# Taking the last 16 tokens out of the expert down products and computing their dots from gathered rows

## The chip, the cores and the metric

The kernel runs on one core of one Trainium2 chip. The metric is the device time of one execution in microseconds (us); the figure shown for a kernel is the median of several runs. A difference of about 0.3% (5.2 us) is what a measurement of this kernel can tell from none.

## The reference

The program is two transformer blocks over 256 tokens of width 1024 (S = 256, D = 1024). All that the change touches lies in the last part, a layer of product-key experts:

```python
def _peer(h, w_q, subkeys, w_down, w_up):
    ...
        v, i = lax.top_k(s, PEER_TOPK)
        cand = (v[..., 0, :, None] + v[..., 1, None, :]).reshape(B, TB, PEER_HEADS, PEER_TOPK * PEER_TOPK)
        ...
        tv, tj = lax.top_k(cand, PEER_TOPK)
        eidx = jnp.take_along_axis(cidx, tj, axis=-1)
        w = jax.nn.softmax(tv, axis=-1)
        u = w_down[eidx]
        a = jax.nn.gelu(jnp.einsum('btd,btpkd->btpk', hblk, u).astype(jnp.float32))
        vv = w_up[eidx]
        return jnp.einsum('btpk,btpkd->btd', (w * a).astype(hblk.dtype), vv)
```

Each token picks 16 of 16,384 experts in each of 8 heads. Of every picked expert its down row (1024 values) is multiplied with the token, the result goes through gelu, is weighted, and scales the expert's up row.

## The kernel before

**Dense products instead of gathers.** The 16,384 experts are 128 tiles of 128 experts. For every tile the kernel computes the down products of all 256 tokens (experts on the partitions, tokens on the columns), so the array `WA` (128 x 128 tiles x 256 tokens) comes to hold gelu(down product) times routing weight, zero where a token did not pick the expert. Then the up products of all 128 tiles are summed in PSUM.

**Weights as pieces.** Down and up rows arrive as a stream of 529 pieces of 128 x 1024 float32 (512 KB), loaded by SyncE into a ring of three buffers (`load_piece`, L178). Each piece is split in two reduced-precision float32 parts: ScalarE copies the high half (`split_high`, L192), and another engine subtracts it from the piece for the low half (`split_low`, L199): GpSimd in the lead described below, VectorE elsewhere. Three pairs of split buffers (AHEAD = 3) stand between these engines and TensorE, and the split of piece q + 3 waits until TensorE has used piece q. A product of two split operands is three matmuls: high x high, high x low, low x high.

**The stages of the expert layer**, in order of time:

1. Key scores. TensorE computes queries and scores, VectorE takes the top 16 of each half.
2. The lead: tiles 0 to FIRST - 1 (FIRST = 36), `lead_tile` (L2359). Per tile `down` (L2312) issues 8 x 3 matmuls of 256 columns (the lines L273, L274 and L277 of `mm3`), ScalarE splits the high half of the tile three ahead and applies gelu into `WA`, and GpSimd makes the low half. The tiles 6 to 29 are in a loop that VectorE takes no part in. VectorE meanwhile finds each token's 16 best pairs and their expert numbers (L2460 to L2516), then waits for ScalarE's exponential (L2518), whose place in ScalarE's own order is behind the loop. Three tiles before the end TensorE turns expert numbers and weights by token (`turn_route`, L2528).
3. The routing steps: 64 steps of 4 tokens (ROUTES = 64). Per step VectorE makes two one-hot arrays (`onehots`, L2557 and L2558), ScalarE weights one (`weights_in`, L2566), TensorE multiplies them (`route_product`, L2575), and ScalarE and VectorE write the resulting weights into `WA` for those 4 tokens. Beside it each step does the down products of one more tile in a wider form, `down_wide` (L2327): per k one matmul of 512 columns (the high half against both parts of the tokens, L2337) and one of 256 (L2341); `whole_tile` (L2352) adds the two halves.
4. The pairs: 28 tiles (100 to 127), each with `down_wide`, gelu and weighing, followed by the up product of another tile (12 matmuls of 512 columns).
5. The up products of the last 100 tiles, then the final norm.

The order on each engine is as written in the program; every engine works its own list in order and waits on semaphores. Before the routing steps the lists read:

```python
    for u in range(FIRST - BODY, FIRST):
        ...
        lead_tile(u, None)
    onehots(1)
    V.wait_ge(s_low, q1 + AHEAD)
```

Of the kernel before, what the change touches and what calls it, by code (L numbers as in the profile page):

```python
# [28 lines left out]
U32 = mybir.dt.uint32  # L29
ALU = mybir.AluOpType  # L30
# [25 lines left out]
FIRST = 36  # L56
TB = 4
ROUTES = S // TB
# [59 lines left out]
def build(nc, a, out):  # L118
# [2189 lines left out]
    I16f = carve(NT, 2 * PH, TOPK)  # L2308
    s_gelu = nc.alloc_semaphore("gelu_done")
    q0 = pos["q"] + 2 * PH  # L2310

    def down(q, s, u, n, first=False):  # L2312

        if not first:
            T.wait_ge(s_gelu, n + (u - 2))

        def products(h, l):
            for k in range(KD):
                last = mm3(bank[4 + u % 3][:, 0:S], (h[:, k * P:(k + 1) * P], l[:, k * P:(k + 1) * P]),
                           (xh[:, k, :], xl[:, k, :]), k == 0, k == KD - 1)  # L2320
            return last
        piece_ops(q, s, products)
# [4 lines left out]
    def down_wide(q, s, v, n):  # L2327

        T.wait_ge(s_gelu, n + (v - 2))
        b = bank[4 + v % 3]  # L2330

        def products(h, l):
            for k in range(KD):
                ks = slice(k * P, (k + 1) * P)

                def both_parts(stop):
                    return T.matmul(b[:, :], h[:, ks], xs[:, k, :, :].rearrange("p a t -> p (a t)"), start=k == 0, stop=stop,  # L2337
                                    skip_group_check=True)

                def high_part(stop):  # L2340
                    return T.matmul(b[:, 0:S], l[:, ks], xh[:, k, :], start=False, stop=stop, skip_group_check=True)  # L2341
# [10 lines left out]
    def whole_tile(g, v, n):  # L2352

        b = bank[4 + v % 3]
        C.activation(g[:, :], b[:, S:2 * S], ACT.Copy).then_inc(s_right, 1)
        V.wait_ge(s_right, n + (v - FIRST + 1))
        V.tensor_tensor(g[:, :], b[:, 0:S], g[:, :], ALU.add).then_inc(s_whole, 1)

    def lead_tile(u, i):  # L2359
        n = 0 if i is None else i * BODY  # L2360
        down(q0 + u, n, u, n, first=i is None and u < 3)
        split(q0 + u + AHEAD, i, low=G)
        C.wait_ge(s_used, n + (q0 + u + 1))
        row = WA[:, u, :] if i is None else WA[:, bass.ds(n + u, 1), :].rearrange("p a t -> p (a t)")
        C.activation(row, bank[4 + u % 3][:, 0:S], ACT.Gelu_apprx_tanh).then_inc(s_gelu, 1)
# [29 lines left out]

    for st in range(2 * PH + 3):
# [46 lines left out]
    with nc.Fori(1, FIRST // BODY - 1, engines=(ENG.PE, ENG.Activation, ENG.Pool)) as i:  # L2443
# [55 lines left out]
    places = (order, place)  # L2499
    dve.wait(ci)  # L2500
# [3 lines left out]
    for w in range(2):  # L2504
        for t in range(NT):
# [9 lines left out]
    W3 = Wt.rearrange("p t h k -> p (t h) k")  # L2515
    s1 = dve.did(V.tensor_tensor(W3, TV, TV[:, :, 0:1].broadcast_to([P, NT * PH, TOPK]), ALU.subtract))  # L2516
    act.wait(s1)
    e_ = act.did(C.activation(Wt, Wt, ACT.Exp))  # L2518
    dve.wait(e_)
    m = dve.did(V.tensor_reduce(wsum, Wt, AX.X, ALU.add))  # L2520
    dve.wait(m)
    m = dve.did(V.reciprocal(wsum, wsum))
    dve.wait(m)
    for t in range(NT):
        wd = dve.did(V.tensor_tensor(Wt[:, t, :, :], Wt[:, t, :, :], wsum[:, t, :].unsqueeze(2).broadcast_to([P, PH, TOPK]),
                                     ALU.mult))

    def turn_route(n_, src, ready, dst):  # L2528

        pe.wait(ready)  # L2530
        for t in range(NT):
            last = T.transpose(bank[1 + n_][:, t * P:(t + 1) * P], src[:, t, :, :].rearrange("p h k -> p (h k)"), ident)
        r_ = pe.did(last)
        act.wait(r_)
        return act.did(C.activation(dst[:, :], bank[1 + n_][:, 0:S], ACT.Copy))
# [46 lines left out]
    def route_copy(g):  # L2582

        lo = FIRST + min(g + 1, ROUTES - 1)
        C.wait_ge(s_wp, g + 1)
        C.activation(WA[:, lo:NE, TB * g:TB * g + TB], by_tile(g)[:, lo:NE, :], ACT.Copy).then_inc(s_wc, 1)

    def route_multiply(g):
# [3 lines left out]
        V.wait_ge(s_wc, g + 1)  # L2592
        V.wait_ge(s_gelu, hi)
# [9 lines left out]
    def late_gelu(g):  # L2603
# [456 lines left out]
```

## Time and profile before

| what | us |
| --- | --- |
| median of 3 runs | 1719.74 |
| lowest and highest run | 1718.23, 1723.38 |
| span of the profiled execution (first to last instruction) | 1718.3 |
| TensorE busy in it | 1692.9 |
| VectorE, ScalarE, GpSimd busy in it | 1283.4, 970.7, 234.7 |

The profile gives the span as the profiled execution's own time and nothing beyond it. The median of the runs is 1.4 us above that span; this is taken for what lies around the span. In the profile PE is TensorE's matmuls, PEld its weight loads, DVE VectorE, ACT ScalarE, POOL GpSimd, SP SyncE; SPq and ACTq are the parts of SyncE and ScalarE that issue DMAs. A group of rows names line, engine, operation, what is written and read with its shape, and for waits the releaser behind an arrow. A matmul's duration overlaps the next one's, so the pace of TensorE is read from starts, not from durations.

### The profile page before, as it was taken

The page shows a single profiled execution, that of the slowest core. Times are in us where ns is not written, and L with a number is a line of the kernel's source. Part 1 is how long each engine was busy: PE and PEld are TensorE (multiplying, and loading weights), DVE is VectorE, ACT ScalarE, POOL GpSimd, SP SyncE. Part 2 cuts the span into 40 slices and gives each one's busy share as a digit, 9 for nine tenths or more (in the row PEclk, how much of TensorE's full clock was granted, in tenths as well). Part 3 has the DMA queues.
Part 4 walks back from the last instruction along what each step waited for, and adds up shares of the span by engine and source line. Part 5 has one row for each costly group of instructions (what it writes and reads, how often), then busy time and mean ns, then how long its engine had stood idle before and what let it go on. Part 6 is the DMA issues. An engine that isn't in the chain of part 4 may idle for free.

```text
span 1718.3 us, 30152 instructions
## 1 busy us (share of the span) xinstructions
PE 1692.9 (99%) x10170; PEld 1497.8 (87%) x10170; DVE 1283.4 (75%) x2549; ACT 970.7 (56%) x1798; POOL 234.7 (14%) x172
## 2 busy tenths in 40 slices
PE   9999999999999999999899999999999999999998
PEld 8888888799888887889899999999988888888886
DVE  5468877867788788867658766889987666666667
ACT  5746554566555544557455548988874544333333
POOL 2120000011100000321117883000000000000000
PEclk9999999999999999999999999999999999999999
DMA  7535767655547686444245555444446555555554
GB/s 243 189 127 156 267 206 281 212 176 202 207 146 268 217 284 243 165 160 140 82 138 170 178 180 169 140 143 148 140 143 193 187 194 185 194 195 193 190 192 146
DMA packets 86579, 317.50 MB, mean 185 GB/s; under 512 B 9664, under 2 KB 9936, under 8 KB 85968
## 3 DMA queue, kind: packets, MB, share of 16 engines
q1 hardware_dynamic: 77328, 279.48, 49.2%
q10 hardware_dynamic: 7200, 25.45, 4.0%
q0 software_dynamic: 1952, 11.25, 1.9%
q8 instruction: 61, 1.00, 0.2%
q14 instruction: 38, 0.31, 0.1%
HBM read 315.08 MB, written 1.05 MB: 184 GB/s over the span
## 4 chain that ended last, share of the span: by engine, by line
PE 69%; DVE 4%; ACT 2%; DMA 2%; issue 1%; POOL 0%; DVEq 0%; SPq 0%; ACTq 0%
PE bank L273 13%; PE bank L277 13%; PE bank L274 13%; PE bank L2337 10%; PE bank L2341 5%; PE bank L1250 4%; PE bank L2575 3%; PE bank L1254 2%; DVE wl L199 1%; DMA ada<-in_w_ada 1%; ACT wh L192 1%; PE bank L622 1%; DMA ring<-in_stream 1%; PE bank L676 1%; PE bank L699 1%
## 5 line engine op out<-in xcount | busy, mean ns | idle before, releaser
L192 ACT ACTIVATE wh<-ring 128x1024 fp32r<-128x1024 f32 x526 | 555.6, 1058 | 537.6 <-PE bank L277 356.1
L199 DVE TENSOR_TENSOR wl<-ring,wh 128x1024 fp32r<-128x1024 f32 x468 | 572.8, 1226 | 279.2 <-ACT wh L192 277.8
L273 PE MATMUL bank<-wh,xs 128*128 128x512 f32 (+1 forms) x780 | 279.5, 358 | 2.0 <-DVE wl L199 0.8
L277 PE MATMUL bank<-wh,xs 128*128 128x512 f32 (+1 forms) x780 | 275.7, 353 | 0.0
L274 PE MATMUL bank<-wl,xs 128*128 128x512 f32 (+1 forms) x780 | 275.4, 353 | 0.0
L2337 PE MATMUL bank<-xs,wh 128*128 128x512 f32 x736 | 250.8, 402 | 0.0
L1250 PE MATMUL bank<-xs,wh 128*128 128x512 f32 x672 | 212.4, 396 | 1.9 <-DVE wl L199 1.9
L273 PE MATMUL bank<-xs,wh 128*128 128x256 f32 x616 | 177.4, 288 | 0.3 <-ACT fox_v L1127 0.2
L277 PE MATMUL bank<-xs,wl 128*128 128x256 f32 x616 | 174.3, 283 | 0.0
L274 PE MATMUL bank<-xs,wh 128*128 128x256 f32 x616 | 174.2, 283 | 0.0
L199 POOL TENSOR_TENSOR wl<-ring,wh 128x1024 fp32r<-128x1024 f32 x57 | 138.4, 2430 | 262.0 <-ACT wh L192 168.4
L273 PEld LDWEIGHTS bank<-wh,xs 128*128 128x128 f32 x780 | 147.4, 189 | 25.5 <-DVE wl L199 2.9
L277 PEld LDWEIGHTS bank<-wh,xs 128*128 128x128 f32 x780 | 147.3, 189 | 20.7
L274 PEld LDWEIGHTS bank<-wl,xs 128*128 128x128 f32 x780 | 147.5, 189 | 20.3 <-issue 0.5
L2341 PEld LDWEIGHTS bank<-xs,wl 128*128 128x128 f32 x736 | 138.5, 188 | 29.3
L1254 PEld LDWEIGHTS bank<-xs,wl 128*128 128x128 f32 x672 | 126.2, 188 | 29.5
L2341 PE MATMUL bank<-xs,wl 128*128 128x256 f32 x736 | 145.1, 279 | 0.0
L1254 PE MATMUL bank<-xs,wl 128*128 128x256 f32 x672 | 132.1, 278 | 0.0
L2337 PEld LDWEIGHTS bank<-xs,wh 128*128 128x128 f32 x736 | 119.1, 189 | 1.1
L273 PEld LDWEIGHTS bank<-xs,wh 128*128 128x128 f32 x616 | 118.1, 192 | 0.8 <-ACT fox_v L1127 0.4
L274 PEld LDWEIGHTS bank<-xs,wh 128*128 128x128 f32 x616 | 118.1, 192 | 0.1
L277 PEld LDWEIGHTS bank<-xs,wl 128*128 128x128 f32 x616 | 117.9, 191 | 0.0
(505 smaller groups left out, 2849.6 us busy)
## 6 DMA issues: line engine op xcount, KB each, us to landing
ring<-in_stream SPq DMA_DIRECT2D x529, 512.0 KB, 3.4
ada<-in_w_ada ACTq DMA_DIRECT2D x48, 512.0 KB, 4.7
rows<-in_rows POOLq DMA_DIRECT2D x1, 2560.0 KB, 11.3
rows<-in_rows POOLq DMA_DIRECT2D x3, 512.0 KB, 5.2
con<-in_early POOLq DMA_DIRECT2D x1, 1374.0 KB, 14.4
x_feature_major<-in_x_fm SPq DMA_DIRECT2D x4, 256.0 KB, 5.9
x<-in_x_tm POOLq DMA_DIRECT2D x1, 1024.0 KB, 5.5
rows<-in_rows POOLq DMA_DIRECT2D x1, 1024.0 KB, 7.5
```

What stands on the lines that cost most here:

```text
L192: C.activation(wh[q % AHEAD][:, :], ring[slot][:, :], ACT.Copy).then_inc(s_high, 1)
L199: low.tensor_tensor(wl[q % AHEAD][:, :], ring[slot][:, :], wh[q % AHEAD][:, :], ALU.subtract).then_inc(s_low, 1)
L273: T.matmul(o, left[0], right[0], start=start, stop=False, skip_group_check=True)
L274: T.matmul(o, left[0], right[1], start=False, stop=False, skip_group_check=True)
L277: return T.matmul(o, left[1], right[0], start=False, stop=stop, skip_group_check=True)
L622: T.matmul(o, v[0], w[:, 0:S], start=first, stop=False, skip_group_check=True)
L676: scored = pe.did(T.matmul(b[:, P:3 * P], q[:, P:2 * P], k, start=True, stop=True, skip_group_check=True))
L1250: return T.matmul(g[:, :], h[:, ks], xs[:, k, :, :].rearrange("p a t -> p (a t)"), start=k == 0, stop=stop, skip_group_check=True)
L1254: return T.matmul(g[:, 0:S], l[:, ks], xh[:, k, :], start=False, stop=stop, skip_group_check=True)
L2337: return T.matmul(b[:, :], h[:, ks], xs[:, k, :, :].rearrange("p a t -> p (a t)"), start=k == 0, stop=stop, skip_group_check=True)
L2341: return T.matmul(b[:, 0:S], l[:, ks], xh[:, k, :], start=False, stop=stop, skip_group_check=True)
L2575: last = T.matmul(bank[g % 4][:, k * P:(k + 1) * P], oh_i[g % 2][:, k, :], oh_j[g % 2][:, k, :], start=True, stop=True, skip_group_check=True)
```

## The change

- `LIVE = 240`: every down product takes 240 columns instead of 256, the wide form 2 x 240 instead of 512. The gelus, copies and weighings of these tiles shrink alike.
- The dots of the 16 tokens left out are made another way. VectorE computes their expert numbers first (the loop over `t` runs 1, 0), ScalarE issues 8 small DMAs (`choose`) that lay out 16 tokens x 8 heads on the 128 partitions, and GpSimd issues 16 indirect DMAs (`gather`), one behind each of 16 lead tiles; each fetches 128 down rows of 4 KB from the new input `down_rows`. VectorE multiplies each gathered 128 x 1024 array with the tokens' own rows and sums along it (`chosen_dot`); TensorE has put those rows into PSUM with 8 matmuls (`own_rows`). In the routing steps 2 to 10 the 128 x 16 dots are turned by 8 DMAs of ScalarE (`dots_by_token`), go through gelu, are turned on TensorE and are multiplied into the routing weights of the 16 tokens; for these tokens the routing steps then write weight times gelu directly.
- FIRST goes from 36 to 45: nine tiles move from the pairs to the lead (19 pairs remain). The loop now covers tiles 6 to 23, tiles 24 to 44 are written out. GpSimd keeps the low halves of the whole lead.
- `onehots(1)` moves behind VectorE's wait for GpSimd's last low half.

```diff
-FIRST = 36
+FIRST = 45
+TAKEN = 16
+LIVE = S - TAKEN
+BY_POOL = 28
...
-                last = mm3(bank[4 + u % 3][:, 0:S], (h[:, k * P:(k + 1) * P], l[:, k * P:(k + 1) * P]),
-                           (xh[:, k, :], xl[:, k, :]), k == 0, k == KD - 1)
+                last = mm3(bank[4 + u % 3][:, 0:LIVE], (h[:, k * P:(k + 1) * P], l[:, k * P:(k + 1) * P]),
+                           (xh[:, k, 0:LIVE], xl[:, k, 0:LIVE]), k == 0, k == KD - 1)
...
-                    return T.matmul(b[:, :], h[:, ks], xs[:, k, :, :].rearrange("p a t -> p (a t)"), start=k == 0, stop=stop,
-                                    skip_group_check=True)
+                    return T.matmul(sides, h[:, ks], xs[:, k, :, 0:LIVE], start=k == 0, stop=stop, skip_group_check=True)
...
+    def own_rows(ready, free):
+
+        pe.wait(ready, free)
+        for k in range(KD):
+            last = T.matmul(own_ps[:, k * P:(k + 1) * P], own[:, k * P:(k + 1) * P], ident, start=True, stop=True,
+                            skip_group_check=True)
+        return pe.did(last)
...
+    def choose():
+
+        act.wait(numbered)
+        for h in range(PH):
+            C.dma_start(chosen[h * TAKEN:(h + 1) * TAKEN, :],
+                        picks_of[P - TAKEN:P, h * TOPK:(h + 1) * TOPK]).then_inc(s_chosen, 16)
+
+    def gather(r):
+
+        if r == 0:
+            G.wait_ge(s_chosen, 16 * PH)
+        if r >= len(rows_of):
+            G.wait_ge(s_dot, r - len(rows_of) + 1)
+        G.indirect_dma_start(rows_of[r % 10], None, a["down_rows"],
+                             bass.IndirectOffsetOnAxis(ap=chosen[:, r:r + 1], axis=0)).then_inc(s_row[r % 10], 16)
+
+    def chosen_dot(r):
+
+        row = rows_of[r % 10]
+        dve.wait(own_done)
+        V.wait_ge(s_row[r % 10], 16 * (r // 10 + 1))
+        V.tensor_tensor_reduce(out=row, in0=row, in1=own_ps, scale=1.0, scalar=0.0, op0=ALU.mult, op1=ALU.add,
+                               accum_out=dots[:, r:r + 1]).then_inc(s_dot, 1)
...
+    choose()
+    for u in range(LOOPED, FIRST):
...
         lead_tile(u, None)
+        if u - LOOPED < TOPK:
+            gather(u - LOOPED)
+        if u == BY_POOL + 1:
+            own_done = own_rows(own_ready, picked)
+            wd = route_weights()
+        if u >= FIRST - TOPK:
+            chosen_dot(u - (FIRST - TOPK))
+    V.wait_ge(s_low, q1 + AHEAD)
     onehots(1)
-    V.wait_ge(s_low, q1 + AHEAD)
...
+        if g == 2:
+            dots_by_token()
+        if g == 5:
+            chosen_ready = chosen_gelu()
+        if g == 8:
+            chosen_turned = chosen_turn(chosen_ready)
+        if g == 10:
+            weighed_in = chosen_weights(chosen_turned, w_in)
```

Three places in the order of the engines' lists. First GpSimd, from the end of the lead's loop (`wl` the low halves, `ring` the pieces; the line numbers of the changed kernel are up to 34 higher here). Before:

```order
L2443 COMPARE_AND_BRANCH
L199 TENSOR_TENSOR wl0<-ring0,wh0 128x1024
L199 TENSOR_TENSOR wl1<-ring1,wh1 128x1024
L199 TENSOR_TENSOR wl2<-ring2,wh2 128x1024
L199 TENSOR_TENSOR wl0<-ring0,wh0 128x1024
```

With the change:

```order
L2477 COMPARE_AND_BRANCH
L203 TENSOR_TENSOR wl0<-ring0,wh0 128x1024
L2569 DMA weighted<-in_down_rows,chosen_rows 128x1024
L203 TENSOR_TENSOR wl1<-ring1,wh1 128x1024
L2569 DMA weighted<-in_down_rows,chosen_rows 128x1024
L203 TENSOR_TENSOR wl2<-ring2,wh2 128x1024
```

The pattern goes on: 16 indirect DMAs alternate with the low halves of tiles 27 to 42, and five low halves follow without one.

Second ScalarE at the same place, before:

```order
L2443 COMPARE_AND_BRANCH
L2518 ACT_TABLE_LOAD
L2518 ACTIVATE weighted<-weighted 128x256
L192 ACTIVATE wh0<-ring0 128x1024
L2365 ACT_TABLE_LOAD
```

With the change:

```order
L2477 COMPARE_AND_BRANCH
L2602 ACT_TABLE_LOAD
L2602 ACTIVATE weighted<-weighted 128x256
L2560 DMA chosen_rows<-weighted 16x16 x8
L196 ACTIVATE wh0<-ring0 128x1024
L2379 ACT_TABLE_LOAD
```

The 8 small DMAs stand between the exponential and the high half of tile 27, and the exponential now comes after tile 23 instead of tile 29.

Third VectorE at the start of the routing steps, before:

```order
L2557 TENSOR_TENSOR onehot_i0<-keep,route_i 128x512 [waits act_done]
L2558 TENSOR_TENSOR onehot_j0<-keep,route_j 128x512
L2557 TENSOR_TENSOR onehot_i1<-keep,route_i 128x512
L2558 TENSOR_TENSOR onehot_j1<-keep,route_j 128x512
L2557 TENSOR_TENSOR onehot_i0<-keep,route_i 128x512 [waits route_product,piece_low]
```

With the change:

```order
L2646 TENSOR_TENSOR onehot_i0<-keep,route_i 128x512
L2647 TENSOR_TENSOR onehot_j0<-keep,route_j 128x512
L2577 ISA weighted,chosen_dots<-weighted,bank 128x1024 [waits gathered5]
L2577 ISA chosen_dots 128x1
L2646 TENSOR_TENSOR onehot_i1<-keep,route_i 128x512 [waits piece_low]
L2647 TENSOR_TENSOR onehot_j1<-keep,route_j 128x512
```

The one-hot arrays of step 1 now wait for GpSimd's last low half (`piece_low`); before, those of step 2 did.

## Rows read from the trace of the kernel before

**Rows 1.** The page: span, TensorE's busy time, the chain that ended last.
```profile
span 1718.3 us, 30152 instructions
PE 1692.9 (99%) x10170; PEld 1497.8 (87%) x10170; DVE 1283.4 (75%) x2549; ACT 970.7 (56%) x1798; POOL 234.7 (14%) x172
PE 69%; DVE 4%; ACT 2%; DMA 2%; issue 1%; POOL 0%; DVEq 0%; SPq 0%; ACTq 0%
```

**Rows 2.** Busy by stretch: PE, PEld, DVE, ACT, POOL; last clock, DMA share, GB/s.
```profile
961.00:1046.00 85.00, 85.00 (x712) 85.00 (x710) 61.33 (x168) 44.25 (x70) 71.12 (x30) 1.00 0.56 180
1047.00:1281.00 234.00, 234.00 (x1527) 211.85 (x1527) 205.43 (x372) 205.80 (x566) 2.85 (x2) 1.00 0.44 145
```

**Rows 3.** Timeline of GpSimd, lead: start, duration, work, count, idle before.
```profile
904.25 7.13 POOL L199 TENSOR_TENSOR wl<-ring,wh 128x1024 fp32r<-128x1024 f32 x3 [0.69 <-ACT wh L192]
...
1000.73 2.40 POOL L199 TENSOR_TENSOR wl<-ring,wh 128x1024 fp32r<-128x1024 f32 x1 [0.48 <-ACT wh L192]
1003.61 2.40 POOL L199 TENSOR_TENSOR wl<-ring,wh 128x1024 fp32r<-128x1024 f32 x1 [0.48 <-ACT wh L192]
...
1038.23 2.41 POOL L199 TENSOR_TENSOR wl<-ring,wh 128x1024 fp32r<-128x1024 f32 x1 [0.48 <-ACT wh L192]
1041.77 8.13 POOL L199 TENSOR_TENSOR wl<-ring,wh 128x1024 fp32r<-128x1024 f32 x3 [1.14 <-ACT wh L192]
```

**Rows 4.** Timeline of TensorE, among the up products and the key scores.
```profile
1285.15 0.39 PE L273 MATMUL bank<-wh,wa_high 128*128 128x512 f32 x1
...
1286.51 0.39 PE L273 MATMUL bank<-wh,wa_high 128*128 128x512 f32 x1
...
801.59 1.87 PE L1965 MATMUL bank<-kc_pair,nqT 128*128 128x30 f32 x16
```

**Rows 5.** The instructions on the tile gelu: duration min/median/max, first and last start.
```profile
L2694 ACT ACTIVATE gelu<-gelu x28: 417/418/418, 1289.4 to 1436.8; 128x256 f32<-128x256 f32 x28
```

**Rows 6.** Timeline of ScalarE at the end of the lead's loop.
```profile
1011.11 1.06 ACT L192 ACTIVATE wh<-ring 128x1024 fp32r<-128x1024 f32 x1 [1.55 <-PE bank L277]
1012.08 0.37 ACT L2365 ACTIVATE weighted<-bank 128x256 f32 x1
...
1029.35 0.37 ACT L2365 ACTIVATE weighted<-bank 128x256 f32 x1
1029.74 1.28 ACT L2518 ACT_TABLE_LOAD   x1
```

**Rows 7.** Groups by line on GpSimd: busy, mean ns, idle before.
```profile
L143 POOL DMA_DIRECT2D weighted<-in_subkeys x2 | 1.2, 579 | 0.9 <-DVE xs L429 0.9
...
L509 POOL TENSOR_TENSOR ln_rstd<-ln_var,nhalf 128x1 f32<-128x1 f32 x8 | 4.5, 558 | 3.9 <-DVE ln_var L507 3.7
...
L2066 POOL TENSOR_TENSOR ret_rstd<-ret_var,nh 128x8 f32<-128x8 f32 x1 | 1.7, 1676 | 3.6 <-DVE ret_var L2062 3.6
```

**Rows 8.** DMA issues from ScalarE: two in a row early on.
```profile
11.04 0.39 ACTq L143 DMA_DIRECT2D keep<-in_keep  x1
11.47 0.45 ACTq L143 DMA_DIRECT2D vec<-in_vec  x1
```

**Rows 9.** The instructions on the tile ada: DMA issues, and a multiply-and-sum over 1024.
```profile
L379 ACTq DMA_DIRECT2D ada<-in_w_ada x48: 334/334/339, 170.5 to 661.6; - x48
L384 DVE CUSTOM_DVE_ANT_0 ada<-ada,silu_c x48: 1215/1218/1226, 177.8 to 668.6; 128x1024 f32<-128x1024 f32 x48
```

**Rows 10.** Timeline of VectorE, choosing the experts, and the first one-hot arrays.
```profile
1014.95 2.29 DVE L2514 TENSOR_REDUCE weighted<-bank 128x128 f32<-128x2048 f32 x1
...
1049.93 0.69 DVE L2557 TENSOR_TENSOR onehot_i<-keep,route_i 128x512 f32<-128x512 f32 x1 [4.73 <-POOL wl L199]
```

**Rows 11.** Routing steps: weighting on ScalarE.
```profile
1054.99 1.27 ACT L2566 ACTIVATE onehot_j<-onehot_j,route_w 128x128 f32<-128x128 f32 x4
```

**Rows 12.** Routing steps: two consecutive routing products on TensorE.
```profile
1057.18 1.05 PE L2575 MATMUL bank<-onehot_j,onehot_i 128*128 128x128 f32 x8
1060.86 1.05 PE L2575 MATMUL bank<-onehot_j,onehot_i 128*128 128x128 f32 x8
```

More of the change, by code:

```diff
@@ L2308, in build @@
     I16f = carve(NT, 2 * PH, TOPK)
+    rows_of = [carve(D) for i in range(10)]
+    own = carve(D)
+    picks_of = carve(PH * TOPK, dt=I32)
+    chosen = sb(peer, "chosen_rows", [P, TOPK], I32)
+    dots = sb(peer, "chosen_dots", [P, TOPK])
+    dots_t = sb(peer, "chosen_dots_by_token", [TAKEN, PH * TOPK])
+    s_chosen = nc.alloc_semaphore("chosen_rows_landed")
+    s_row = [nc.alloc_semaphore(f"gathered{i}") for i in range(10)]
+    s_dot = nc.alloc_semaphore("chosen_dot_made")
+    s_dots_t = nc.alloc_semaphore("chosen_dots_turned")
     s_gelu = nc.alloc_semaphore("gelu_done")
@@ L2394, in feature_pair, with own_copies @@
         return (s_used, q + 2)
+    own_f = own.rearrange("p (k h t) -> p k h t", k=KD, h=PH)
+    def own_copies():
+        parts_of = [part[:, :, LIVE:S].unsqueeze(2).broadcast_to([P, KD, PH, TAKEN]) for part in (xh, xl)]
+        return dve.did(V.tensor_tensor(own_f, parts_of[0], parts_of[1], ALU.add))
+    own_ps = banks[:, 2 * HALF:4 * HALF]
+    def own_rows(ready, free):
[4 more added lines that the diff above has]
+        return pe.did(last)
+    dve.wait(operand["high"][KD - 1], operand["low"][KD - 1])
+    own_ready = own_copies()
     for st in range(2 * PH + 3):
@@ L2517, in build, with chosen_gelu, chosen_turn, chosen_weights @@
+    def chosen_gelu():
+        C.wait_ge(s_dots_t, 16 * PH)
+        return act.did(C.activation(dots_t[:, :], dots_t[:, :], ACT.Gelu_apprx_tanh))
+    def chosen_turn(made):
+        pe.wait(made)
+        return pe.did(T.transpose(bank[7][:, 0:TAKEN], dots_t[:, :], ident[0:TAKEN, 0:TAKEN]))
+    def chosen_weights(turned, ready):
+        dve.wait(turned, ready)
+        return dve.did(V.tensor_tensor(wT[:, LIVE:S], wT[:, LIVE:S], bank[7][:, 0:TAKEN], ALU.mult))
     act.wait(s1)
     e_ = act.did(C.activation(Wt, Wt, ACT.Exp))
-    dve.wait(e_)
@@ L2520, in build, with route_weights @@
[L2520 to L2526, printed above, removed]
+    def route_weights():
+        dve.wait(e_)
+        m = dve.did(V.tensor_reduce(wsum, Wt, AX.X, ALU.add))
+        dve.wait(m)
+        m = dve.did(V.reciprocal(wsum, wsum))
+        dve.wait(m)
+        for t in range(NT):
+            wd = dve.did(V.tensor_tensor(Wt[:, t, :, :], Wt[:, t, :, :],
+                                         wsum[:, t, :].unsqueeze(2).broadcast_to([P, PH, TOPK]), ALU.mult))
+        return wd
@@ L2641, in build @@
         if g + 1 < ROUTES:
+            if TB * (g + 1) == LIVE:
+                act.wait(weighed_in)
             weights_in(g + 1)
```

66 lines of the change are left out of this document (43 added, 23 removed).

## The prediction

> **What bounds the kernel now.** I read the page first: TensorE is busy for 1692.9 of the 1718.3 us span and holds 69% of the chain that ended last [rows 1]. So I ask of each stage whether TensorE still sets its pace, and what comes next behind it. [...] The timelines give the reserves. In the lead a low half of GpSimd starts every 2.88 us, takes 2.40, and waits 0.48 for ScalarE; run without waits, three took 7.13, so 2.38 each [rows 3]. ScalarE in turn waits 1.55 us per tile for TensorE [rows 6]. GpSimd is thus next in line in the lead, with 0.5 us to spare per tile. In the routing steps, 3.68 us apart, the weighting ends at 1056.26 and TensorE needs it at 1057.18: 0.9 us to spare [rows 11, 12].
>
> The sum is made against the span of 1718.3 us; 1.4 us are added to come to the median of 1719.74.
>
> **Columns taken away.** Six matmuls of 512 columns start within 1.36 us, 0.227 each [rows 4]; a lead tile's 24 of 256 columns fill 2.88 us, 0.120 each [rows 3]. The difference is 0.416 ns per column, over a fixed 13 ns. A tile loses 8 x 48 = 384 columns in either form, so 0.160 us, and 128 tiles lose **20.5 us**. This counts in full where TensorE sets the pace, at 2.72 us per lead tile and 3.52 per routing step.
>
> **Nine tiles moved to the lead.** A pair lasts (1436.8 - 1289.4) / 27 = 5.46 us [rows 5], of which 12 x 0.227 = 2.72 are the up product; so the wide form costs 2.74 where the lead form costs 2.88. Nine tiles add **1.3 us**.
>
> **GpSimd's 16 indirect DMAs.** The trace of before has no indirect DMA. Call g the time that one holds GpSimd. From below the nearest row is its issue of a plain DMA with 128 partitions, 0.58 us; from above its longest small operation, 8 values per partition, 1.68 us; nothing lets it come out below a plain issue, since it also has to read 128 numbers [rows 7]. I take **g = 1.0**, near the plain issue, plus most of an operation on one value per partition (0.56) for reading them [rows 7]. Even at 0.58 a tile then costs GpSimd 2.96 us against TensorE's 2.72, so GpSimd sets the pace from tile 27 on, once the stock of ready pieces is gone. When:
>
> - Tile 29's gelu runs at 1029.35, with the exponential's table load behind it; tile 23, after which the changed lists go on, has its gelu at 1012.08 and ended at 1011.0 [rows 6]. The 24 tiles being 0.16 shorter, these become 1008.2 and 1007.2.
> - Behind it ScalarE does the table load (1.28 us) and the exponential (0.4): 1010.3. Then come the 8 small DMAs. Two issues in a row don't overlap, 11.04 to 11.43 and 11.47 to 11.92 [rows 8]; at 0.33 each [rows 9], seven hold the list for 2.3 us. The high half of tile 27 ends at 1013.7. The expert numbers it waits for are not late: VectorE's whole choice ended at 1017.2 [rows 10], the half needed here two of its four rounds earlier.
> - GpSimd then has 17 low halves (27 to 43) and 16 DMAs before tile 43 can start: 1013.7 + 17 x 2.38 + 16 g = 1054.2 + 16 g. TensorE alone would be there at 1007.2 + 19 x 2.72 + 0.7 = 1059.6, 0.7 being the three turns of routing numbers (the step from 1038.23 to 1041.77 is that much over 2.88) [rows 3]. The delay is 16 g - 5.4: **10.6 us** at 1.0.
>
> Hidden in this wait are the 8 matmuls of `own_rows` (16 passes as in a routing product, at 0.11 us, so 1.8 us [rows 12]); without it they would cost that. The 16 dots, 1.22 us each by the like operation [rows 9], run on a VectorE that stood idle until 1031 in the old program, and GpSimd waits for dot 0 only at its DMA 10. SyncE's queue gets nothing new, but the transfers do: a tile now fetches 0.52 + 0.52 MB. The lead moved 180 GB/s at a share of 0.56 [rows 2], so some 320 GB/s when full, 3.27 us per tile: just under GpSimd's 3.38, and covered as long as g is near 1.
>
> **One-hot arrays behind the last low half.** GpSimd's low half of tile 47 ends 4 x 2.38 = 9.5 us after tile 43 starts. Then VectorE needs two operations of 0.69 [rows 10] and ScalarE 1.27 [rows 11]: 12.1. TensorE would want them after tiles 43, 44, one routing product (0.9) and the wide tile 45 (2.7): 9.0. I count **3.1 us**, once. VectorE's first splits are queued behind this wait too, but their tile is three further on.
>
> **Dots turned in step 2.** Another 8 issues of ScalarE, 2.3 us against the 0.9 to spare: **1.4 us**, once. The gelu of the dots and their turn on TensorE: **0.4**.
>
> **The sum**: -20.5 + 1.3 + 10.6 + 3.1 + 1.4 + 0.4 = -3.7 us; 1714.6 as a span, **1716 us** as a median. With g open it is -19.7 + 16 g: zero at g = 1.23. Since 0.3% is 5.2 us, this is a forecast of **no measurable change**, and g decides: below 0.91 it is faster, above 1.56 slower.
>
> **Weight loads against columns.** The records of 30 columns at 801.59 start (1.87 - 0.27) / 15 = 0.107 us apart, 0.27 being the last one's own length [rows 4]: however few columns, a matmul with new weights comes no faster. A matmul of 240 columns at 0.113 lies 6 ns above that floor, so I count the saving whole. [...]
>
> **Rivals.**
>
> 1. *GpSimd issues an indirect DMA almost like a plain one* (g = 0.58 to 0.9). [...] Against it: the numbers must be fetched first. At 0.58 the sum is -10.4, **1709 us**, and 1706 if the small DMAs cost ScalarE nothing in either place (2.3 and 1.4 less). The transfers would then have to go beyond 320 GB/s.
> 2. *GpSimd is held much longer* (g = 1.7, the upper bound). The same mechanism at the same place, between tiles 27 and 43: -19.7 + 27.2 = +7.5, **1727 us**. It decides from 1.56 on. For it: one value per partition alone costs GpSimd 0.56. Against it: it would be three plain issues. If the stream's pieces come late beside the gathered rows, a few us more: 1731.
> 3. *The short matmuls get no faster* because their pace is the weight load, 0.120 us at 240 columns as at 256. Then only the 83 x 8 wide ones save, 664 x 13.3 ns = 8.8 us in place of 20.5; the lead stays at 2.88 us, so GpSimd delays it by 3 us less, and the sum is +5.0: **1725 us**, at the edge of slower. For it: 256 columns and a load of 128 take almost the same time. Against it: the spacing of 0.107 above.
> 4. *A matmul of the reduced type under 256 columns is run like a plain float32 one.* Every row of this type has 256 or 512 columns, so nothing shows it. Plain passes of 128 columns come 0.11 us apart, two per product [rows 12], so 1.73 ns per column: 240 would take 0.42 us instead of 0.12, and 45 x 24 + 83 x 8 = 1744 matmuls would add some 520 us: **2240 us**.
>
> **Chances and range.** The forecast, g between 0.91 and 1.56, gets 0.36. Rival 1 gets 0.36 too, since a plain issue is the only like row. Rival 2 gets 0.19, rival 3 0.06 and rival 4 0.03; rival 3, at the edge, counts half as the same and half as slower. So 0.36 faster, 0.39 the same, 0.25 slower, and the forecast's own range is 1714.6 to 1724.9. The whole range runs from 1706, rival 1 with cheap issues on ScalarE, to 1731, rival 2 with late pieces; it leaves out rival 4 and both tails.
>
> **What would show it.** Right: low halves of GpSimd about 3.4 us apart in tiles 27 to 42, TensorE waiting for them; lead matmuls 0.113 apart before that; one gap of about 3 us before routing product 1; steps of 3.5 us after it; some 2 us of ScalarE taken by issues before tile 27 and in step 2. Wrong: GpSimd at or under 2.9 us per tile (rival 1), over 4 (rival 2), unchanged spacing in the first lead tiles (rival 3) or a lead several times as long (rival 4). Waits of VectorE for landing rows, or of ScalarE for stream pieces, would mean that the transfers bind, which I hold to be just covered.

## The result: slower by about half a per cent

The changed kernel takes 1728.61 us (median of 4 runs, 1728.06 to 1734.04), the kernel before 1719.28 beside it. The ratio is **1.0056, 95% interval 1.0038 to 1.0074**: slower by 6.5 to 12.7 us. The forecast was no measurable change, 1716 us. The profiled execution spans 1727.0 us, 8.7 more than that of before; the sums further down are made between such spans.

First the page of the changed kernel: span, busy times, the chain that ended last by engine.

```profile
span 1727.0 us, 30270 instructions
PE 1682.8 (97%) x10259; PEld 1495.5 (87%) x10259; DVE 1288.8 (75%) x2557; ACT 962.8 (56%) x1787; POOL 270.9 (16%) x197
PE 58%; DVE 10%; POOL 3%; ACT 3%; DMA 3%; issue 2%; ACTq 0%; DVEq 0%; SPq 0%
```

TensorE has 10.1 us less to do than in [rows 1] and its share of the chain fell from 69% to 58%: the work went, waits came. They came into stages in which TensorE had none to speak of: in both stretches of [rows 2] it is busy for the whole time (85.00 and 234.00 us), at a granted clock of 1.00. Which ones, the list of TensorE's waits tells, for whom and how long (total, times, longest):

```profile
PE bank L277 <- POOL wl L203: 8.3, 12, 1.8
PE bank L2666 <- ACT onehot_j L2655: 7.4, 3, 3.7
```

Neither line exists in the kernel before. GpSimd's own timeline answers to [rows 3]: the low halves of tiles 24 and 25, then tile 27, one round of the steady pattern, and the end.

```profile
1003.15 2.40 POOL L203 TENSOR_TENSOR wl<-ring,wh 128x1024 fp32r<-128x1024 f32 x1 [0.27 <-ACT wh L196]
1005.83 2.42 POOL L203 TENSOR_TENSOR wl<-ring,wh 128x1024 fp32r<-128x1024 f32 x1 [0.28 <-ACT wh L196]
...
1014.65 2.37 POOL L203 TENSOR_TENSOR wl<-ring,wh 128x1024 fp32r<-128x1024 f32 x1 [3.73 <-ACT wh L196]
...
1039.57 2.41 POOL L203 TENSOR_TENSOR wl<-ring,wh 128x1024 fp32r<-128x1024 f32 x1
1042.13 0.95 POOL L2569 DMA_INDIRECT weighted<-in_down_rows,chosen_rows  x1 [0.16 <-issue]
1043.11 2.40 POOL L203 TENSOR_TENSOR wl<-ring,wh 128x1024 fp32r<-128x1024 f32 x1
...
1071.34 9.90 POOL L203 TENSOR_TENSOR wl<-ring,wh 128x1024 fp32r<-128x1024 f32 x4
1084.12 2.38 POOL L203 TENSOR_TENSOR wl<-ring,wh 128x1024 fp32r<-128x1024 f32 x1 [2.88 <-ACT wh L196]
```

Before the gathers a tile comes every 2.68 us (2.88 before the change): TensorE took the columns. With a gather it is 3.54 (1043.11 - 1039.57), 0.95 in the indirect DMA and 0.16 ahead of it, and GpSimd never waits for another engine there: it sets the pace. Two waits of its own frame the stretch, 3.73 us before tile 27 and 2.88 before the last low half. ScalarE's and VectorE's timelines tell of both (`ACTq` is the issuing of DMAs):

```profile
1007.69 1.25 ACTq L2560 DMA_DIRECT2D chosen_rows<-weighted  x2
1008.97 1.24 ACTq L2560 DMA_DIRECT2D chosen_rows<-weighted  x1
1010.23 3.17 ACTq L2560 DMA_DIRECT2D chosen_rows<-weighted  x5
1013.51 1.06 ACT L196 ACTIVATE wh<-ring 128x1024 fp32r<-128x1024 f32 x1 [3.09 <-PE bank L281]
...
1081.82 1.28 ACT L2655 ACTIVATE onehot_j<-onehot_j,route_w 128x128 f32<-128x128 f32 x4 [3.30 <-DVE onehot_j L2647]
1083.01 1.04 ACT L196 ACTIVATE wh<-ring 128x1024 fp32r<-128x1024 f32 x1
...
1096.68 1.16 ACTq L2584 DMA_DIRECT2D chosen_dots_by_token<-chosen_dots  x2
1097.87 3.81 ACTq L2584 DMA_DIRECT2D chosen_dots_by_token<-chosen_dots  x6
```

```profile
1075.82 3.20 DVE L2646 TENSOR_TENSOR onehot_i<-keep,route_i 128x512 f32<-128x512 f32 x1
1078.95 2.84 DVE L2647 TENSOR_TENSOR onehot_j<-keep,route_j 128x512 f32<-128x512 f32 x1
```

A small DMA holds ScalarE 3.17 / 5 = 0.63 us, twice what I took from [rows 9]; tile 27's high half stands behind eight of them (the profile puts its 3.09 us down to TensorE, which had long been done). Part of that cost was hidden: in ScalarE's list the eight come behind the exponential, but in the trace the first began at 1007.69, while the table load of that exponential began only at 1008.71. At the end, the one-hot arrays of step 0 take 3.20 and 2.84 us in place of 0.69, while GpSimd's low halves run back to back. ScalarE waits for them, its high half of tile 47 stands behind, and GpSimd's last low half behind that. The routing products on TensorE, answering to [rows 12], show what it cost:

```profile
1083.15 2.08 PE L2666 MATMUL bank<-onehot_j,onehot_i 128*128 128x128 f32 x8 [3.67 <-ACT onehot_j L2655]
1089.19 1.16 PE L2666 MATMUL bank<-onehot_j,onehot_i 128*128 128x128 f32 x8 [0.76 <-ACT onehot_j L2655]
1092.83 1.05 PE L2666 MATMUL bank<-onehot_j,onehot_i 128*128 128x128 f32 x8
1096.37 1.05 PE L2666 MATMUL bank<-onehot_j,onehot_i 128*128 128x128 f32 x8
1103.05 1.82 PE L2666 MATMUL bank<-onehot_j,onehot_i 128*128 128x128 f32 x8 [2.99 <-ACT onehot_j L2655]
1108.29 1.05 PE L2666 MATMUL bank<-onehot_j,onehot_i 128*128 128x128 f32 x8
```

A step lasts from one product to the next; the steady one is 3.54 us. Step 0 lasts 6.04; step 3 lasts 6.68 behind the eight issues that turn the dots, and step 4 5.24, with no wait in it (the last section shows why).

### The profile page after: what moved, and what is told of

The parts are those of the page before. It is cut to its first block, busy times and chain, and to the rows that moved or that the text cites. A ratio compares the mean times of both kernels' runs of the same rounds, so it can differ in the third digit from the quotient of the medians.

```text
span 1727.0 us, 30270 instructions
## 1 busy us (share of the span) xinstructions
PE 1682.8 (97%) x10259; PEld 1495.5 (87%) x10259; DVE 1288.8 (75%) x2557; ACT 962.8 (56%) x1787; POOL 270.9 (16%) x197
## 3 DMA queue, kind: packets, MB, share of 16 engines
q8 instruction: 64, 1.05, 0.3%
HBM read 323.47 MB, written 1.05 MB: 188 GB/s over the span
## 4 chain that ended last, share of the span: by engine, by line
PE 58%; DVE 10%; POOL 3%; ACT 3%; DMA 3%; issue 2%; ACTq 0%; DVEq 0%; SPq 0%
PE bank L277 11%; PE bank L281 11%; PE bank L278 11%; PE bank L2352 8%; PE bank L2355 4%; PE bank L2666 3%; DVE wl L203 3%; POOL wl L203 2%; PE bank L1254 2%; DMA ada<-in_w_ada 1%; ACT wh L196 1%; DMA ring<-in_stream 1%; PE bank L1258 1%; DVE ada L388 1%; POOL weighted L2569 1%
## 5 line engine op out<-in xcount | busy, mean ns | idle before, releaser
L277 PE MATMUL bank<-wh,xs 128*128 128x512 f32 (+1 forms) x816 | 293.5, 360 | 1.9 <-DVE wl L203 0.9
L281 PE MATMUL bank<-wh,xs 128*128 128x512 f32 (+1 forms) x816 | 289.7, 355 | 0.0
L278 PE MATMUL bank<-wl,xs 128*128 128x512 f32 (+1 forms) x816 | 289.5, 355 | 0.0
L2352 PE MATMUL bank<-xs,wh 128*128 128x480 f32 x664 | 219.3, 392 | 0.0
L1254 PE MATMUL bank<-xs,wh 128*128 128x512 f32 x672 | 212.5, 396 | 2.7 <-DVE wl L203 2.7
L277 PE MATMUL bank<-xs,wh 128*128 128x240 f32 (+1 forms) x688 | 196.4, 285 | 8.6 <-POOL wl L203 8.3
L203 POOL TENSOR_TENSOR wl<-ring,wh 128x1024 fp32r<-128x1024 f32 x66 | 159.2, 2416 | 260.0 <-ACT wh L196 164.8
L278 PE MATMUL bank<-xs,wh 128*128 128x240 f32 (+1 forms) x688 | 192.2, 279 | 0.0
L281 PE MATMUL bank<-xs,wl 128*128 128x240 f32 (+1 forms) x688 | 192.2, 279 | 0.0
L281 PEld LDWEIGHTS bank<-wh,xs 128*128 128x128 f32 x816 | 154.1, 189 | 21.9
L277 PEld LDWEIGHTS bank<-xs,wh 128*128 128x128 f32 x688 | 131.8, 192 | 11.4 <-issue 8.6
L1258 PE MATMUL bank<-xs,wl 128*128 128x256 f32 x672 | 132.1, 278 | 0.0
L278 PEld LDWEIGHTS bank<-xs,wh 128*128 128x128 f32 x688 | 131.8, 192 | 0.1
L2355 PE MATMUL bank<-xs,wl 128*128 128x240 f32 x664 | 128.4, 275 | 0.0
L2352 PEld LDWEIGHTS bank<-xs,wh 128*128 128x128 f32 x664 | 107.8, 192 | 0.8
```

Of the source, the lines that this page charges most:

```text
L203: low.tensor_tensor(wl[q % AHEAD][:, :], ring[slot][:, :], wh[q % AHEAD][:, :], ALU.subtract).then_inc(s_low, 1)
L277: T.matmul(o, left[0], right[0], start=start, stop=False, skip_group_check=True)
L278: T.matmul(o, left[0], right[1], start=False, stop=False, skip_group_check=True)
L281: return T.matmul(o, left[1], right[0], start=False, stop=stop, skip_group_check=True)
L1254: return T.matmul(g[:, :], h[:, ks], xs[:, k, :, :].rearrange("p a t -> p (a t)"), start=k == 0, stop=stop, skip_group_check=True)
L1258: return T.matmul(g[:, 0:S], l[:, ks], xh[:, k, :], start=False, stop=stop, skip_group_check=True)
```

## The experiments

Theory: the columns brought what was summed, and the loss lies in engines that are held (GpSimd by gathers, ScalarE by small issues, VectorE by GpSimd), each of which can be undone alone. The main rival: the transfers, 1.05 MB per tile with a gather, set the pace. All ratios are to the kernel before, measured again beside each group of runs (its median went from 1719.28 to 1720.70); 0.1% is 1.7 us. Each diff shows the lines that carry the edit, not all of it.

### Columns alone, with a lead of 36 tiles

All calls of `choose`, `gather`, `own_rows`, `chosen_dot`, `dots_by_token` and what follows them are taken out.

```diff
-FIRST = 45
+FIRST = 36
...
-        if u - LOOPED < TOPK:
-            gather(u - LOOPED)
...
-        if u >= FIRST - TOPK:
-            chosen_dot(u - (FIRST - TOPK))
```

> This kernel takes only the columns away (240 in place of 256, lead of 36 tiles again); the dots of the last 16 tokens are left out of the output, and with them every gather, small DMA and dot. My theory (the columns bring what was summed, and the loss is all in what was added): the saving is 36 x 0.20 + 64 x 0.15 + 28 x 0.12 = 20 us, ratio to the kernel before 0.988. Rival (another engine takes over as soon as TensorE needs less): at most 10 us, ratio 0.994 or above.

Measured: 1705.24 us, ratio 0.991 (0.9893 to 0.9926), some 15 us. Short of 20, far from the rival's 0.994.

### Columns alone, with the lead of 45 tiles

The same without the first two lines of that diff.

> As the columns alone, but with the lead of 45 tiles, GpSimd making all its low halves and the one-hot arrays of step 1 behind the last of them; again without the dots of the last 16 tokens in the output. My theory: nine tiles in the lead form cost what they cost in a pair (+0.5 us), and without gathers GpSimd keeps up at 2.68 us per tile; so within 2 us of the columns alone, ratio to the kernel before 0.988 to 0.990. Rival (the longer lead itself costs, since GpSimd's last low half and VectorE's one-hot arrays come late whatever else is done): 3 us or more above the columns alone.

Measured: 1702.92 us, ratio 0.9908 (0.9885 to 0.9931). The longer lead costs nothing that shows. This is the changed kernel without its rows, and the measure for all that follows: the rows cost 1728.61 - 1702.92 = **25.7 us**. Its routing product 1:

```profile
1068.24 1.16 PE L2665 MATMUL bank<-onehot_j,onehot_i 128*128 128x128 f32 x8 [2.56 <-ACT onehot_j L2656]
```

The wait of 2.56 us is that for the one-hot arrays behind the last low half, forecast at 3.1. The run with the lead of 36 tiles has it too, also 2.56. It was in my sum but not in the 20 us of the expectation, and is the larger part of what is missing there. Most of the rest is the step behind it: 5.21 us in the lead of 36 tiles, at a granted clock of 0.58 from 1048.6 to 1052.7 us, against 3.65 with 45 tiles.

### VectorE makes the low halves beside the gathers

```diff
-        lead_tile(u, None)
+        if u == BY_POOL:
+            V.wait_ge(s_low, q0 + BY_POOL + AHEAD)
+        lead_tile(u, None, low=V if u >= BY_POOL else G)
```

> The changed kernel, with the low halves of tiles 31 to 47 made by VectorE in place of GpSimd, so that GpSimd has only the gathers from there on. [...] Rival (a tile with gather fetches 1.05 MB, at some 300 GB/s that is 3.5 us, so the transfers set the pace): pace unchanged at 3.5 us, time 1725 to 1729.

Measured: 1721.86 us, ratio 1.0008 (0.9998 to 1.0019), clear of the changed kernel's interval, though by the medians 6.8 us and so a little short of the 8 to 16 that I had counted on, from tiles 2.7 to 3.1 us apart once GpSimd's 0.95 + 0.16 us are off the list of low halves. Between 1042 and 1062 us the low halves came 3.16 us apart, just over the 3.1. The transfers moved 396 GB/s there, so the rival's 300 is no limit. With GpSimd out of the way the one-hot arrays of step 0 are short again, as VectorE's timeline shows; but TensorE waited for them as long as before:

```profile
1074.09 0.69 DVE L2646 TENSOR_TENSOR onehot_i<-keep,route_i 128x512 f32<-128x512 f32 x1
1074.69 0.68 DVE L2647 TENSOR_TENSOR onehot_j<-keep,route_j 128x512 f32<-128x512 f32 x1
...
1076.74 1.55 PE L2666 MATMUL bank<-onehot_j,onehot_i 128*128 128x128 f32 x7 [4.16 <-ACT onehot_j L2655]
```

The wait before product 0 is 4.16 us here and 3.67 in the changed kernel. VectorE was busy for 14.25 of the 15 us from 1060 on, with low halves and dots in turn, and the arrays stood behind them. So the gain of this edit lies in the lead, and the length of the arrays was not all that held product 0; their place in VectorE's list did too.

### Gathers of a sixteenth of the bytes

```diff
-        G.indirect_dma_start(rows_of[r % 10], None, a["down_rows"],
+        G.indirect_dma_start(rows_of[r % 10][:, 0:64], None, a["down_rows"].rearrange("n (a d) -> (n a) d", d=64),
```

> The changed kernel, with each gather fetching 64 values per partition in place of 1024 (32 KB in place of 512 KB, rows of a narrower view, so that the dots of the last 16 tokens in the output are not those of their experts). My theory (GpSimd is held by the descriptors, not by the bytes): the indirect DMA still takes 0.95 us and the low halves still start 3.5 us apart; only the late stream pieces at the end go away, 1724 to 1729. Rival (the transfers set the pace): the low halves start 2.7 to 2.9 us apart and the time falls by 10 us or more, to 1718 or below.

The dots shrink with them, to 64 columns. Measured: 1729.03 us, ratio 1.0048 (1.0031 to 1.0065), the same as the changed kernel. GpSimd's timeline has the pattern unchanged, 3.53 us apart:

```profile
1036.86 0.96 POOL L2569 DMA_INDIRECT weighted<-in_down_rows,chosen_rows  x1 [0.16 <-issue]
1037.83 2.40 POOL L203 TENSOR_TENSOR wl<-ring,wh 128x1024 fp32r<-128x1024 f32 x1
1040.39 0.96 POOL L2569 DMA_INDIRECT weighted<-in_down_rows,chosen_rows  x1 [0.16 <-issue]
```

So the hold does not go by bytes, and the transfers did not set the pace of the changed kernel. My detail that the wait before the last low half would go with the late pieces was wrong: it was 3.50 us here. The hold ends before the rows are there: from issue to landing the median was 5.6 us with 512 KB and 3.5 with 32, while the instruction held GpSimd for 0.95 and 0.96. What it does go by, the descriptors of my theory or something else, no run here shows: every gather has 128 rows.

### The dots' eight DMAs spread over the steps 2 to 16

```diff
-        if g == 2:
-            dots_by_token()
+        if g % 2 == 0 and 2 <= g <= 2 * PH:
+            dots_by_token(g // 2 - 1)
```

> The changed kernel, with the 8 small DMAs that turn the dots issued one in every second routing step (2 to 16) in place of all in step 2, and gelu, turn and multiply in steps 20, 23 and 25. My theory (each issue holds ScalarE 0.61 us; 8 in a row took 4.97 us out of one step, and TensorE then ran at half clock for some 4 us): the steps of 6.68 and 5.24 us become 3.53, 4.9 us in all, less up to 1.3 where an issue does not fit beside a step's own work; time 1722.5 to 1725. Rival (that step is long because of the dots that come late, or of the first late tiles, not of the issues): 1727.5 to 1729.

Measured: 1723.35 us, ratio 1.0016 (1.0006 to 1.0025): 5.3 us by the medians, as expected. What the theory started from stands in the changed kernel's trace: the eight issues on `chosen_dots_by_token` took 0.515 to 0.613 us each, median 0.611, and 1.16 + 3.81 = 4.97 in sum; behind them the granted clock was 0.56 from 1103.0 to 1106.9 us, 0.50 in the middle of it (1104 to 1106). The routing products 3 and 4 now follow at the steady pace:

```profile
1097.81 1.05 PE L2666 MATMUL bank<-onehot_j,onehot_i 128*128 128x128 f32 x8
1101.34 1.05 PE L2666 MATMUL bank<-onehot_j,onehot_i 128*128 128x128 f32 x8
```

### One-hot arrays of steps 0 and 1 after tile 32

```diff
-        if u == FIRST - 3:
+        if u == BY_POOL + 2:
...
-        if u == FIRST - 1:
+        if u == BY_POOL + 4:
             onehots(0)
+            onehots(1)
             weights_in(0)
+            weights_in(1)
```

> The changed kernel, with the turns of the routing numbers after tile 30 and the one-hot arrays and weightings of steps 0 and 1 both after tile 32, so that nothing of it stands behind the late dots or behind GpSimd's last low half. [...] Rival (GpSimd's backlog of low halves would have held TensorE there anyway): the same time shows up as waits for the low halves of tiles 45 to 47, 1726 to 1728.6.

Measured: 1724.47 us, ratio 1.0016 (1.0006 to 1.0026): 4.1 us by the medians, between the 6 to 9 that I had counted on and the rival, and 7 by the ratios. TensorE no longer waits before products 0 and 1, but 10.9 us for GpSimd in place of 8.3 (0.71 and 0.70 of it before the two tiles behind tile 27, where the changed kernel ran at half clock and did not wait), and 1.78 before product 2, since GpSimd's last low half still came late. This time ScalarE's high half of that tile had waited 3.55 us for a piece of the stream (at 1082.82 us).

### The three edits together

VectorE's low halves, spread dots and early one-hot arrays.

> The three edits together: VectorE makes the low halves of tiles 31 to 47, the one-hot arrays of steps 0 and 1 come early, the 8 turning DMAs are spread. My theory (the losses are separate holds and add up): from the 1721.9 us of the first edit alone, 7.6 us of waits before routing products and some 2 us of half clock behind them go: 1710 to 1714. Rival (with GpSimd out of the way the transfers bind at 3.1 us per tile, and what is freed elsewhere comes back as waits for stream pieces): 1717 or more.

Measured: 1712.38 us, ratio 0.9956 (0.9939 to 0.9972): faster than before. By the medians the edits alone gained 6.8, 5.3 and 4.1, in sum 16.2, and together 16.2. (By the ratios the sum is 22 and the whole 17, with some 3 us of uncertainty on each; that the holds add up is shown no closer than this.)

### SyncE issues the sixteen small DMAs

```diff
-        act.wait(numbered)
+        load_to((q0 + 28) // RING)
+        sp.wait_ge(*numbered)
         for h in range(PH):
-            C.dma_start(chosen[h * TAKEN:(h + 1) * TAKEN, :],
+            sp.dma_start(chosen[h * TAKEN:(h + 1) * TAKEN, :],
```

> As the three edits together, but SyncE issues the 16 small DMAs, the first eight as soon as the expert numbers are there (1005.7 us in the changed kernel's profile, ScalarE began 2 us later), the second eight at the start of the routing steps. My theory (ScalarE's eight issues before tile 27 cost TensorE a wait of 1.79 us and half clock for 3.4 us): high half of tile 27 some 3 us earlier, no half clock there, 1707 to 1711. Rival (eight issues on the queue that loads the stream delay its pieces by as much, 8 x 0.6 = 5 us against a ring of three): no better than the spread version, or worse by up to 4 us.

Measured: 1723.96 us, ratio 1.0029 (1.0017 to 1.0042), 11.6 us worse than the three edits. The rival, and more than it said. SyncE's queue:

```profile
1005.90 5.91 SPq L2568 DMA_DIRECT2D chosen_rows<-weighted  x8
1012.15 59.95 SPq L182 DMA_DIRECT2D ring<-in_stream  x21
1079.86 4.95 SPq L2593 DMA_DIRECT2D chosen_dots_by_token<-chosen_dots  x8
```

The stream stood still for 5.91 and 4.95 us; TensorE then waited 3.5 us once for a low half and 8.0 before routing product 2. The second pause was longer than its issues, as the list of SyncE's waits shows, since SyncE first stood waiting for the last dot:

```profile
SPq L2593 <- DVE chosen_dots L2585: 7.6, 1, 7.6
```

So of this pause more is the wait than the issuing, and what the issues alone would cost on that queue is not shown. A hold moved to another queue is still a hold, and so is a wait.

### The three edits, with gathers of a sixteenth of the bytes

The three edits and the line of the narrow gathers above.

> The kernel with the three edits, its gathers fetching 64 values per partition in place of 1024 (rows of a narrower view, so the dots of the last 16 tokens in the output are not those of their experts). My theory (once GpSimd is out of the way, the 1.05 MB per tile set the pace of the tiles with gathers at about 3.1 us): these tiles come 2.7 us apart and the time falls by 4 to 7 us, to 1705 to 1708.5. Rival (VectorE's and ScalarE's own lists set that pace): 1711 or more.

Measured: 1712.63 us, ratio 0.995 (0.9935 to 0.9965): no change. My theory fell: with GpSimd free the bytes cost little here. In the full version the transfers moved 410 GB/s between 1040 and 1050 us. TensorE's waits are nearly the same in both: 1.8 before tile 27 and 1.3 over the next two, some 1.9 for the turn of the weights, which stood behind VectorE's low halves, and behind the weightings 1.57 in the full version, 0.57 with the narrow gathers. That 1.0 us may be the bytes'; the narrow run lost it again at half clock (0.50 between 1033 and 1036 us, where the full one held 1.00). The other waits are places in the engines' lists, and those are what is left.

### Those places mended, and a longer lead

First two issues behind each of the tiles 24 to 27, gathers from tile 28 on, weights' turn and weightings moved:

```diff
-    choose()
...
+        if u - LOOPED < PH // 2:
+            choose(u - LOOPED)
+        if 0 <= u - BY_POOL < TOPK:
+            G.wait_ge(s_used, q0 + u)
+            gather(u - BY_POOL)
```

> The three edits, and: ScalarE issues two of the first eight small DMAs behind each of the tiles 24 to 27, the gathers stand behind tiles 28 to 43, each released by TensorE's progress, the weights' turn no longer waits for VectorE, and the weightings of steps 0 and 1 stand 3 and 5 tiles behind their one-hot arrays. My theory (two issues of 0.63 us fit into ScalarE's 1.3 us of spare time per tile): no wait of TensorE before tile 27 and no half clock there, 3 to 4 us less than with the three edits: 1708 to 1710. Rival (the gathers start later, and the same bytes in fewer tiles bind more): 1712 or more.

Measured: 1712.81 us, ratio 0.9951 (0.9936 to 0.9967), no gain, as the rival said. The trace shows both halves of it: TensorE waits nowhere between 1010 and 1050 us, but the last gathers now stand just before the routing steps:

```profile
1059.30 1.06 ACT L196 ACTIVATE wh<-ring 128x1024 fp32r<-128x1024 f32 x1 [4.68 <-DMA ring<-in_stream]
...
1061.76 0.35 PE L277 MATMUL bank<-xs,wh 128*128 128x240 f32 x1 [2.11 <-DVE wl L203]
...
1080.96 1.43 PE L2666 MATMUL bank<-onehot_j,onehot_i 128*128 128x128 f32 x8 [3.85 <-ACT onehot_j L2655]
```

The first wait goes back to a piece of the stream, for which ScalarE waited 4.68 us: here the transfers do bind, beside the gathers. The second is for arrays of VectorE that stand behind the last dots; it is followed by half clock (0.50 between 1082.5 and 1084.5 us) and a step of 5.23. Then room for them:

```diff
-FIRST = 45
+FIRST = 51
...
-    rows_of = [carve(D) for i in range(10)]
+    rows_of = [carve(D) for i in range(8)]
...
-        if 0 <= u - BY_POOL < TOPK:
-            G.wait_ge(s_used, q0 + u)
-            gather(u - BY_POOL)
+        for r in range(TOPK):
+            if u == BY_POOL + r * 5 // 4:
+                G.wait_ge(s_used, q0 + u)
+                gather(r)
```

> As the kernel just before, but with a lead of 51 tiles, so that the 16 gathers lie over 19 tiles (one behind tile 28 + 5r/4, rounded down) and the last dots do not stand directly before the routing steps; 8 buffers in place of 10. My theory (transfers bind only as far as a tile fetches more than some 330 GB/s times 2.68 us): pace of about 2.8 us, 1704 to 1707.5. Rival (each further tile in the lead costs more than in a pair): 1709 or more.

Measured: **1705.69 us, ratio 0.9911 (0.9896 to 0.9927)**, the best version that computes everything: 23 us under the changed kernel, some 15 under the kernel before, and level with the columns alone (0.9908). Busy times by stretch (PE, PEld, DVE, ACT, POOL; clock, DMA share, GB/s) answer to [rows 2]:

```profile
961.00:1082.00 121.00, 120.50 (x1078) 120.26 (x1077) 100.30 (x216) 63.69 (x101) 73.51 (x39) 1.00 0.74 260
1082.00:1310.00 228.00, 227.70 (x1546) 211.66 (x1545) 214.50 (x383) 201.72 (x566) 0.00 (x0) 1.00 0.45 152
```

TensorE is idle for 0.5 us of the lead and 0.3 of the routing steps. The longer lead, the wider spacing and the order of the dots were changed at once, so which of them brought the 7 us is not shown. Nor does any run show a limit at the 330 GB/s of the theory: the version above moved 336 and 330 from 1050 to 1060 and from 1060 to 1070 us, beside its wait for a piece, but with the three edits the transfers moved 394 between 1050 and 1060 us while TensorE never waited. Last, this lead with the eight issues at once again and wider gathers:

```diff
+    choose()
...
-        if u - LOOPED < PH // 2:
-            choose(u - LOOPED)
...
-            if u == BY_POOL + r * 5 // 4:
+            if u == LOOPED + r * 3 // 2:
```

> As the lead of 51 tiles, but with the eight small DMAs issued at once again and the gathers earlier and further apart (behind tile 24 + 3r/2). My theory: the eight issues cost what they cost in the changed kernel (TensorE's wait of 1.8 us and half clock behind it, 3 to 4 us), the wider spacing gives 1 to 2 us back: 1705 to 1710. Rival (the issues never mattered, the transfers did): below the version with spread issues.

Measured: 1707.5 us, ratio 0.9928 (0.9912 to 0.9943), within what the theory said, though without the half clock it counted on (1.00 from 1014 to 1030 us). TensorE waits 2.7 us for GpSimd's low halves again, but the interval overlaps that of the version above: the 1.8 us between them are not shown.

## Why the prediction was wrong, point by point

| term of the sum | forecast | measured |
| --- | --- | --- |
| columns, nine tiles, one-hot arrays of step 1 | -20.5 + 1.3 + 3.1 = -16.1 | -17.4 (1700.9 - 1718.3, spans) |
| GpSimd's delay, up to routing product 1 | +10.6 | +20.95 (1089.19 - 1068.24) |
| dots turned and their gelu | +1.4 + 0.4 | +4.86 (6.68 + 5.24 - 2 x 3.53) |
| sum | -3.7 | +8.4 (spans: +8.7) |

Each span is that of one execution, and they reach the lead at different times: its first low half starts at 901.16 us before, at 902.11 in the changed kernel and at 899.90 with the columns alone. Little of the change stands ahead of that, and executions with the same lists up to there differ as much (900.40 with the narrow gathers). So 1.3 of the -17.4 and 2.2 of the 20.95 are differences of the start; counted from there it is -16.1, as forecast, and 18.7 against 10.6.

- **Columns: right.** Lead tiles came at 2.68 (2.72 forecast), steps at 3.53 to 3.54 (3.52). Rivals 3 and 4 are out. 2.68 / 24 is 0.1117 us per matmul of 240 columns, 8 ns under that of 256 where I had counted 7. The floor, though, lies higher than I read it: of the 16 records of 30 columns the first two start 0.03 us apart and the others 0.1117, and from the second of eight of 64 columns (at 783.04 us, before) on it is 0.112 as well. So 240 columns come at that spacing, not 6 ns above it.
- **GpSimd sets the pace: right, and g was nearly right.** 0.95 and 0.16 of issue make 1.11 for my 1.0. GpSimd reached the end of its last low half at 1086.50, where my own working gives 1013.7 + 21 x 2.38 + 16 = 1079.7. The 6.8 between them: 0.95 from a later start; 2.6 from g and from low halves of 2.40; 3.3 at the end, of which 2.88 is the wait shown above. Further, TensorE alone would have been ready at 1068.24 - 2.56 = 1065.7, and I had it at 1068.6; 0.8 of that is the pace of these tiles, and the rest was there at tile 23 already (its gelu ran at 1005.99 there, against 1008.2 forecast).
- **The step that failed outright: "One-hot arrays behind the last low half ... I count 3.1 us, once."** As far as it went it was right (2.56 with the columns alone). But I priced the arrays at 0.69 from a row in which GpSimd was done, and looked only at step 1. Those of step 0 stood behind dots 13 and 14 and beside GpSimd's last low halves, where they took 3.20 and 2.84, and the chain one-hot, weighting, high half, low half ran into GpSimd's own list: 2.88 us before the last low half. The trace of before held the price, in the arrays made beside GpSimd:

```profile
1039.07 2.11 DVE L2557 TENSOR_TENSOR onehot_i<-keep,route_i 128x512 f32<-128x512 f32 x1 [6.35 <-ACT route_j L2535]
...
1042.31 2.90 DVE L2558 TENSOR_TENSOR onehot_j<-keep,route_j 128x512 f32<-128x512 f32 x1
```

  Without GpSimd beside them they take 0.69 and 0.68; that is shown. How much of TensorE's 3.67 us was their length and how much their place behind the dots is not: with short arrays and VectorE's list full it still waited 4.16.
- **The other: "at 0.33 each".** That row was the issue of one large load at a time, and [rows 8] beside it already had 0.39 and 0.45; eight small ones in a row took 0.61 to 0.63 each on ScalarE and 5.91 / 8 = 0.74 on SyncE. In step 2 that was 4.97 us against 0.9 to spare, and the step after the stall ran at half clock. Spreading them removed it.
- **Not counted at all: the clock behind a stall.** See the last section.
- **"The transfers are just covered": the measure was off, the sense right.** I put the full rate at 320 GB/s; 410 were moved with the three edits (1040 to 1050 us). My sign for it misled: ScalarE waited 129.6 us for pieces of the stream (87.7 before) and VectorE 21.9 for landing rows, but with a sixteenth of the bytes the time stayed.
- **Rival 2 had nearly the time (1727), not the cause:** it needed g = 1.7.

So of the 12.4 us between forecast and span, some 7 came from small holds standing in a row (0.95, 3.3 and 3.1), 2.6 from g and the low halves, and about 1 from the start of this execution; the rest is not traced. The one unknown price on which I had set the chances decided little.

## What to carry to other kernels

When a change adds work to engines that have time to spare, read each new instruction's hold from a row of the same kind and count (several in a row, beside the same neighbours), and follow what stands behind it in that engine's list. Spread the holds one per step, below the spare time of a step, and keep the last of them away from the point where stages meet. Moving them to another queue can only help if nothing with a deadline is queued there.

## What the runs showed of the hardware

**An operation of VectorE can take several times as long beside GpSimd.** In the changed kernel one-hot operations, which read two arrays of SBUF, took 0.68 to 0.69 us once GpSimd was done and 2.84 to 3.20 beside low halves run back to back. The dots, which read one array of SBUF and one of PSUM, took 1.21 to 1.22 in either case; no run here changes only where an operand lies. What holds VectorE up beside GpSimd these rows do not tell; they give the price.

**TensorE's clock can fall behind a short stall.** Busy times by stretch of the changed kernel (columns as above), behind the wait of 1.79 us before tile 27 and behind the wait of 2.99 in the routing steps; from 1000 to 1015.1 us the clock was 1.00.

```profile
1018.20:1021.40 3.20, 3.20 (x16) 3.20 (x16) 2.74 (x5) 0.47 (x2) 3.02 (x3) 0.50 0.86 305
1103.00:1106.90 3.90, 3.85 (x16) 3.64 (x17) 2.21 (x5) 3.72 (x13) 0.00 (x0) 0.56 0.00 0
```

At 0.50 the lead's matmuls of 240 columns started 0.213 us apart (1018.41 to 1021.19 us), at 1.00 0.112 (1013.09 to 1015.10). In the lead it cost nothing, since GpSimd set the pace; in the routing steps it made the step of 5.24 us, 1.7 over the steady one. Step 0, behind the wait of 3.67, ran at 0.50 too (1083 to 1086 us), at no cost, since product 1 waited for its arrays anyway. It does not follow every stall: behind the same wait before tile 27 the three edits together (1.88 us) and the narrow gathers (1.76 us) held 1.00. Which stalls it follows these runs do not tell.
